# The router ahead of the expert passes: a shorter chain to the positions, expert weights from ranks, unread products in TensorE's holes

## The reference, cut to what matters

```python
p_group = softmax(t @ wg_r + bg_r)                 # 4 groups
g_val, g_idx = top_k(p_group, 1)
e_logits = (t @ we_r + be_r).reshape(-1, 4, 4)     # 4 experts in each group
sel = e_logits[token, g_idx]                       # the 4 logits of the own group
top_v, top_i = top_k(sel, 2)
top_w = softmax(top_v)                             # weights of the two best experts
combine = one_hot(g_idx) * g_val  x  top_w at top_i
for e in range(16):
    out += combine[:, e] * ((silu(t @ w_gate[e]) * (t @ w_up[e])) @ w_down[e])
```

## Time and profile before

| what | us |
|---|---|
| median of 3 runs | 1613.51 |
| lowest and highest run | 1607.58, 1614.62 |
| span of the profiled execution | 1608.3 |
| TensorE busy in it | 1567.1 |

### The profile page before, as it was taken

One profiled execution on the slowest core, in us unless ns is written; L12 is line 12 of the kernel. 1 busy time (PEld: TensorE's weight loads), 2 busy tenths in 40 slices (PEclk: granted clock), 3 DMA queues, 4 the chain that ended last, 5 costly groups with the idle time before them and its releaser, 6 DMA issues.

```text
span 1608.3 us, 29082 instructions
## 1 busy us (share of the span) xinstructions
PE 1567.1 (97%) x11814; PEld 1471.9 (92%) x11814; DVE 1138.0 (71%) x1424; ACT 855.9 (53%) x1056; POOL 63.4 (4%) x53
## 2 busy tenths in 40 slices
PE   6999999999999999999999999999999989999998
PEld 6999998889999999998888999989999978888886
DVE  7655587766555765569777655578688679889887
ACT  5534454664433643345566433376445467767765
POOL 0000021000000000002100000020210000000000
PEclk9999999999999999999999999999999999999999
DMA  8666744136565576674315555646543759898992
GB/s 274 206 197 186 184 142 125 44 123 209 184 201 183 178 222 196 188 182 131 110 55 182 176 191 183 189 131 185 157 123 114 261 202 359 318 361 317 340 343 101
DMA packets 243781, 311.64 MB, mean 194 GB/s; under 512 B 51940, under 2 KB 183588, under 8 KB 243700
## 3 DMA queue, kind: packets, MB, share of 16 engines
q1 hardware_dynamic: 243088, 309.57, 60.1%
q10 hardware_dynamic: 612, 0.96, 0.2%
HBM read 306.97 MB, written 1.05 MB: 192 GB/s over the span
## 4 chain that ended last, share of the span: by engine, by line
PE 86%; DVE 7%; ACT 4%; DVEq 2%; issue 1%; DMA 1%; SPq 0%; ACTq 0%
PE psum L412 20%; PE psum L414 20%; PE psum L413 20%; PE psum L2740 3%; PE psum L2739 3%; PE psum L2741 3%; PE psum L2765 2%; PE psum L2766 2%; PE psum L2767 2%; DVE unit_low L404 2%; ACT unit_high L398 1%; PE psum L2685 1%; PE psum L1020 1%; PE psum L903 1%; DVEq L2247 1%
## 5 line engine op out<-in xcount | busy, mean ns | idle before, releaser
L404 DVE TENSOR_TENSOR unit_low<-unit_raw,unit_high 128x2048 fp32r<-128x2048 f32 (+1 forms) x186 | 425.8, 2291 | 208.5 <-ACT unit_high L398 208.4
L398 ACT ACTIVATE unit_high<-unit_raw 128x2048 fp32r<-128x2048 f32 (+1 forms) x186 | 346.9, 1869 | 134.0 <-PE psum L414 133.5
L412 PE MATMUL psum<-UH,unit_high 128*128 128x256 f32 x1120 | 319.4, 285 | 6.4 <-DVE UL L458 4.6
L413 PE MATMUL psum<-UL,unit_high 128*128 128x256 f32 x1120 | 316.1, 282 | 0.0
L414 PE MATMUL psum<-UH,unit_low 128*128 128x256 f32 x1120 | 315.8, 282 | 0.0
L2476 DVE TENSOR_TENSOR unit_low<-unit_raw,unit_high 128x2048 fp32r<-128x2048 f32 x96 | 215.5, 2285 | 20.8 <-ACT unit_high L2472 20.7
L412 PEld LDWEIGHTS psum<-UH,unit_high 128*128 128x128 f32 x1120 | 213.2, 190 | 9.2 <-DVE unit_low L404 5.2
L414 PEld LDWEIGHTS psum<-UH,unit_low 128*128 128x128 f32 x1120 | 213.2, 190 | 0.0
L413 PEld LDWEIGHTS psum<-UL,unit_high 128*128 128x128 f32 x1120 | 212.4, 190 | 0.1
L412 PE MATMUL psum<-U2H,unit_high 128*128 128x256 f32 x704 | 197.1, 280 | 1.4 <-DVE U2L L458 1.2
L413 PE MATMUL psum<-U2L,unit_high 128*128 128x256 f32 x704 | 196.3, 279 | 0.0
(11 more groups left out here) (501 smaller groups left out, 2913.4 us busy)
## 6 DMA issues: line engine op xcount, KB each, us to landing
unit_raw<-in_ffn_wg SPq DMA_DIRECT2D x44, 1024.0 KB
unit_raw<-in_ffn_wu SPq DMA_DIRECT2D x44, 1024.0 KB
unit_raw<-in_ffn_wd SPq DMA_DIRECT2D x44, 1024.0 KB
unit_raw<-in_w_in SPq DMA_DIRECT2D x32, 1024.0 KB
unit_raw<-in_expert_w_gate SPq DMA_DIRECT2D x32, 1024.0 KB, 7.2
unit_raw<-in_expert_w_up SPq DMA_DIRECT2D x32, 1024.0 KB, 8.1
unit_raw<-in_expert_w_down SPq DMA_DIRECT2D x32, 1024.0 KB, 6.7
unit_raw<-in_w_out SPq DMA_DIRECT2D x10, 1024.0 KB
```

The costliest lines, as they stand in the source:

```text
L398: act.activation(high[s][:, 0:w], raw[s][:, 0:w], ACT.Copy).then_inc(unit_high, 1)
L404: dve.tensor_tensor(low[s][:, 0:w], raw[s][:, 0:w], high[s][:, 0:w].bitcast(F32), ALU.subtract).then_inc(unit_low, 1)
L412: pe.matmul(dst, wh, xh, start=start, stop=False, skip_group_check=True)
L413: pe.matmul(dst, wh, xl, start=False, stop=False, skip_group_check=True)
```

## The change

Nine things change:

- `first_max` goes. For the group, the comparison with the maximum and the multiplication by the tie weights become one instruction for each of the two token tiles, and the last comparison writes `OH` itself. A second one writes the same to `RT`.
- The gathering of the own group's expert logits (a product of 32 values and a sum) moves from the chain of positions to after `plan`. A maximum over the four and a subtraction join it there, all ahead of the split of unit 1.
- TensorE gets unread products of 128x512 (in `router_pe`): six after the logits, three after the counts, three after the gather. Nobody reads what they write.
- The exponential is one instruction for both softmaxes, after ScalarE's evacuation of both halves instead of ahead of the split of unit 2, and the second one is gone.
- VectorE evacuates both halves and then splits unit 2 (before: half, unit 2, half).
- VectorE splits unit 4 ahead of the weights.
- The weights: an expert is kept when fewer than two others rank above it; its weight is its exponential over the sum of the kept ones. 12 instructions in place of 22.
- In the first pass TensorE gathers the weights between units 4 and 5, instead of after unit 3. Other passes are as before.
- The constants have 16 more columns.

```diff
+            def unread_products(n):
+                for _ in range(n):
+                    pe.matmul(psum[:, 1, :], high_x[0][:, 0:P], high_x[0][:, 0:512], start=True, stop=True, skip_group_check=True)
+            unread_products(6)
             pe.wait_ge(EM.sem, EM.at("group"))
...
+            unread_products(3)
             pe.wait_ge(EM.sem, EM.at("position"))
...
             gather_pe(pe, 0)
+            unread_products(3)
...
             expert_high(act, 0, G2, 1, used(G2, EU - 1))
-            act.wait_ge(EM.sem, EM.at("g_sub"))
-            act.activation(RT[:, :, 24:28], RT[:, :, 24:28], ACT.Exp).then_inc(BM.sem, BM.inc("g_exp"))
             expert_high(act, 0, G2, 2)
             evacuate_act(act, 0)
+            act.wait_ge(EM.sem, EM.at("g_sub"))
+            act.activation(RT[:, :, 24:32], RT[:, :, 24:32], ACT.Exp).then_inc(BM.sem, BM.inc("g_exp"))
             expert_high(act, 0, G2, 3)
             expert_high(act, 0, G2, 4)
-            act.wait_ge(EM.sem, EM.at("t_sub"))
-            act.activation(RT[:, :, 84:85], RT[:, :, 84:85], ACT.Exp).then_inc(BM.sem, BM.inc("t_exp"))
...
-            first_max(c(0, 4), 20, 28, 22, 32)
-            dve.drain()
-            dve.tensor_copy(OH[:, :, :], c(32, 36)).then_inc(EM.sem, EM.inc("group"))
-            dve.tensor_tensor(c(24, 28), c(0, 4), wide(20), ALU.subtract).then_inc(EM.sem, EM.inc("g_sub"))
+            dve.tensor_reduce(c(20), c(0, 4), AX, ALU.max)
+            dve.drain()
+            for n in range(2):
+                dve.scalar_tensor_tensor(out=RT[:, n, 28:32], in0=RT[:, n, 0:4], scalar=RT[:, n, 20:21], in1=K[:, K_TIE],
+                                         op0=ALU.is_ge, op1=ALU.mult)
+            dve.drain()
+            dve.tensor_reduce(c(22), c(28, 32), AX, ALU.max)
+            dve.drain()
+            dve.tensor_tensor(OH[:, :, :], c(28, 32), wide(22), ALU.is_equal).then_inc(EM.sem, EM.inc("group"))
+            dve.tensor_tensor(c(32, 36), c(28, 32), wide(22), ALU.is_equal)
...
             dve.drain().then_inc(EM.sem, EM.inc("plan"))
+            dve.tensor_tensor(c(24, 28), c(0, 4), wide(20), ALU.subtract)
+            dve.tensor_tensor(c(40, 56).rearrange(four, g=4), ...)
+            dve.drain()
+            dve.tensor_reduce(c(56, 60), c(40, 56).rearrange("p n (g e) -> p n e g", g=4), AX, ALU.add)
+            dve.drain()
+            dve.tensor_reduce(c(60), c(56, 60), AX, ALU.max)
+            dve.drain()
+            dve.tensor_tensor(c(28, 32), c(56, 60), wide(60), ALU.subtract).then_inc(EM.sem, EM.inc("g_sub"))
             expert_low(dve, G2, 1)
-            evacuate_dve(dve, 0, lambda: expert_low(dve, G2, 2))
+            evacuate_dve(dve, 0)
+            expert_low(dve, G2, 2)
             expert_low(dve, G2, 3)
+            expert_low(dve, G2, 4)
+            # is_gt, is_ge, times K_LESS, max, sum: the rank of each of the four
...
             dve.wait_ge(BM.sem, BM.at("g_exp"))
-            # the two first maxima of the four expert logits and their weights: 22 instructions
+            dve.scalar_tensor_tensor(out=c(112, 116), in0=c(96, 100), scalar=1.5, in1=c(28, 32), op0=ALU.is_lt, op1=ALU.mult)
+            # two sums, product, reciprocal, times RS[2:4], times the kept exponentials
...
             dve.wait_ge(QM.sem, QM.at("position_b"))
             dve.tensor_copy(POSB[:, :], psum[:, 3, 0:T])
-            expert_low(dve, G2, 4)
...
-            def projection(bank, g, j, kind, q):
+            def slot_weights():
+                pe.wait_ge(EM.sem, EM.at("comb"))
+                ...
+            def projection(bank, g, j, kind, q, first=False):
                 for u in range(2):
+                    if first and j == 1 and kind == 0 and u == 1:
+                        slot_weights()
```

More of the change, by code:

```diff
@@ L92 @@
 K_IOTAC = _take(1)
+K_LESS = _take(16)
 K_COLS = _off
@@ L128, in constants @@
     c[:, K_IOTAC] = i[:, None]
+    c[:, K_LESS] = (i[None, 0:4] < i[0:4, None]).astype(np.float32).reshape(1, 16)
     c[:, K_TIE] = np.array([4, 3, 2, 1], np.float32)
@@ L1634, in build @@
                       "sc3", "yo2", "yd2", "yt2", "yz2", "scn2", "yn2", "sc_low2", "scn3", "sc_low3", "uly2"]
-                   + ["ss_sum", "group", "g_sub", "position", "plan", "t_sub", "comb"])
+                   + ["ss_sum", "group", "position", "plan", "g_sub", "comb"])
         HM = Marks(sem("hybrid_pool"), ["res", "dt_s", "dA", "xdec0", "xdec1", "xd1", "sdec", "yz1", "xd2"])
@@ new lines, in router_dve @@
+            own_ = c(56, 60).unsqueeze(3).to_broadcast([P, 2, 4, 4])
+            dve.tensor_tensor(c(64, 80).rearrange(four, g=4), other, own_, ALU.is_gt)
+            dve.tensor_tensor(c(80, 96).rearrange(four, g=4), other, own_, ALU.is_ge)
+            dve.drain()
+            dve.tensor_tensor(c(80, 96), c(80, 96), K[:, K_LESS].unsqueeze(1).to_broadcast([P, 2, 16]), ALU.mult)
+            dve.drain()
+            dve.tensor_tensor(c(64, 80), c(64, 80), c(80, 96), ALU.max)
+            dve.drain()
@@ L2638, in router_dve @@
+            dve.tensor_reduce(c(96, 100), c(64, 80).rearrange(four, g=4), AX, ALU.add)
+            dve.drain()
             dve.wait_ge(BM.sem, BM.at("g_exp"))
-            dve.tensor_reduce(c(23), c(24, 28), AX, ALU.add)
+            dve.scalar_tensor_tensor(out=c(112, 116), in0=c(96, 100), scalar=1.5, in1=c(28, 32), op0=ALU.is_lt, op1=ALU.mult)
+            dve.tensor_reduce(c(117), c(24, 28), AX, ALU.add)
             dve.drain()
-            dve.reciprocal(c(23), c(23))
+            dve.tensor_reduce(c(116), c(112, 116), AX, ALU.add)
@@ L2642, in router_dve @@
             dve.drain()
-            dve.tensor_tensor(RT[:, :, 23], RT[:, :, 23], RS[:, 2:4], ALU.mult)
-            first_max(c(56, 60), 60, 64, 61, 68)
+            dve.tensor_tensor(c(118), c(116), c(117), ALU.mult)
             dve.drain()
-            dve.tensor_scalar(c(72, 76), c(68, 72), 3 * NEG, None, ALU.mult)
+            dve.reciprocal(c(118), c(118))
             dve.drain()
-            dve.tensor_tensor(c(72, 76), c(72, 76), c(56, 60), ALU.add)
+            dve.tensor_tensor(RT[:, :, 119], RT[:, :, 118], RS[:, 2:4], ALU.mult)
@@ L2649, in router_dve @@
             dve.drain()
[L2650 to L2665, removed]
+            dve.tensor_tensor(c(92, 96), c(112, 116), wide(119), ALU.mult).then_inc(EM.sem, EM.inc("comb"))
             dve.wait_ge(QM.sem, QM.at("position_b"))
             dve.tensor_copy(POSB[:, :], psum[:, 3, 0:T])
-            expert_low(dve, G2, 4)
@@ L2698, in evacuate_act, with evacuate_dve @@
                 ins.then_inc(ug_high, 1)
-        def evacuate_dve(dve, q, between=lambda: None):
+        def evacuate_dve(dve, q):
             for half in range(2):
-                if half:
-                    between()
                 dve.wait_ge(ug_high, 2 * q + (half + 1))
@@ L2727, in expert_pe @@
             last = (GROUPS - 1) + pe.value_load(PLAN[0:1, 0:1], min_val=0, max_val=1)
-            def projection(bank, g, j, kind, q):
+            def slot_weights():
+                pe.wait_ge(EM.sem, EM.at("comb"))
+                for n in range(2):
+                    mm = pe.matmul(psum[:, W_B, 0:4], SEL[:, n, :], RT[:, n, 92:96], start=(n == 0), stop=(n == 1))
+                mm.then_inc(w_gathered, 1)
+            def projection(bank, g, j, kind, q, first=False):
                 for u in range(2):
+                    if first and j == 1 and kind == 0 and u == 1:
+                        slot_weights()
                     e = unit_of(j, kind, u)
@@ L2783, in one_pass @@
                     pe.wait_ge(silu, 4 * q + (EB + j))
-                    projection(G_B, g, j, 0, q)
+                    projection(G_B, g, j, 0, q, first)
                     transposes(j - 1, q)
```

20 lines of the change are left out of this document (5 added, 15 removed).

## The result

The changed kernel took 1613.71 us (median of 20 runs, 1611.52 to 1618.78), the kernel before 1607.78 (median of 20 runs beside them; one of these took 3951.4 us, the other 19 took 1607.07 to 1614.62). The ratio is 1.0029, 95% interval 1.0022 to 1.0036: 4.7 us slower. That is inside the 0.5% that I had called no change, but it is a real loss, on the side that I had not forecast.

What follows compares the result with a forecast made beforehand. It took TensorE's chain of waits through the router to bound the kernel. The terms 1.42 + 0.4 + 1.59 - 0.44 - 0.3 = 2.67 us, taken off the 1613.5 median, gave 1610.8, range 1604.8 to 1614.6.

Steps and rivals of the forecast that it cites:

- the sum: Router to unit 6: earlier start 1.42, `UL` wait 0.4, unit 4 wait 1.59, less gather 0.44 and stall 0.3: 2.67 us.
- shifts that no row speaks of: Leftover case for effects nowhere in the profile rows, given no size; chance 0.03.
- The chain to the positions: Router, group's maximum to positions: `OH` comes 0.33 us earlier, everything up to L2676 about 0.37 us earlier.
- The unread products and the gather: Router: unread products fill TensorE's holes, the clock stays up, and the gather's second half ends at 1300.0 instead of 1303.0.
- What is late next: Start of first pass: unit 1's split starts 0.5 us later than before, yet TensorE begins 1.42 us earlier.
- The first 48 products, the weights, their gather: First pass: products take 11.3 us, not 11.70; unit 4's wait goes; gather costs 0.44 us; unit 6 stalls 0.3 us.
- The clock falls all the same: Rival in the router: the clock drops despite unread products, TensorE begins 0.3 to 0.9 us later, median 1611.4; chance 0.33.
- Transfers or splits hold the passes: Rival in the passes: loads or VectorE set the pace, TensorE stalls later by what it won, time stays 1613.5; chance 0.11.
- The weights come late: Rival in the first pass: TensorE waits for `comb`, slower if later than 1318.4, median 1614.5 at 1 us beyond; chance 0.03.

Runs made afterwards that it cites:

- Experiments 1: The kernel before with only the 16 unread columns of constants, tiles behind `K` 64 bytes further: 1616.04 us, ratio 1.0038.
- experiment 5: The changed kernel with the tiles behind `K` 192 bytes further, 256 bytes in all from their old place: 1606.85 us, ratio 0.9987.
- experiment 7: The kernel before with the 16 unread columns and the tiles behind `K` 256 bytes from their old place: 1609.78 us, ratio 0.9997.
- experiment 4: The changed kernel with tiles behind `K` 64 bytes further still (128 in all) and without its twelve unread products: 1614.56 us, ratio 1.0033.
- Experiment 6: experiment 5 with the expert-logit instructions between VectorE's evacuation halves and unit 6 split before the wait for the weights: 1606.21 us, ratio 0.9976.
- experiment 3: The changed kernel with the tiles behind `K` 32 bytes further, 96 bytes in all from their old place: 1613.22 us, ratio 1.0025.
- experiment 11: experiment 5 with the weights' gather back in its old place after unit 3, one execution: 1605.71 us.
- experiment 12: Experiment 6 with the weights' gather back after unit 3 and unit 6's split behind the wait again: 1606.07 us, ratio 0.9982.

## Why the prediction was wrong, step by step

**The step that failed** is one sentence of the sum: "The moved instructions and the 16 columns of constants are in these steps or under them". For the instructions that held. The columns I costed at nothing, since no engine works on them for long. I didn't follow what they push along. I had every tile behind `K` in the code in front of me, and no entry for their addresses in the sum, only 0.03 for "shifts that no row speaks of". The entry should have been about +6.5 us, what the 2112 products of `U2H` and `U2L` took more. Experiments 1, 5 and 7 show it: the columns without the rest cost 6.1, with the shift brought to 256 bytes they cost nothing that can be told from zero, and the changed kernel then gains 2.1.

**The base was off too.** I subtracted 2.67 from 1613.5, the median of three runs. The median of 20 is 1607.8. The span of 1608.3 that I had for the profiled execution pointed lower than 1613.5: time less span is 1.8 us in all later profiled executions, which makes 1610.1. That is still 2.3 above the median, but 5.2 us between the median of three and this span were a sign that two of the three runs were high, and not something to add to the forecast. The forecast of 1610.8 came near 1613.7 by luck, by two errors that partly cancel: a base 5.7 too high and a missing loss.

**The chain to the positions:** right. Forecast 0.33 for `OH` and 0.37 for the positions; measured 0.30 and 0.33.

**The unread products and the gather:** right for this execution. The clock stayed at 1.00, the holes are 0.8, 0.6 and 0.3 where I had 1.0, 0.8 and 0.6, and the 32 products took 3.54 from first to last start. Without the unread ones unit 6 comes 1.0 later (experiment 4). That the clock stays up was luck in part: in three of seven executions it didn't.

**What is late next:** right. The split of unit 1 starts 0.61 later against the common point (forecast 0.5), TensorE waits for `UL` behind it, and starts 1.38 earlier (forecast 1.42). Experiment 6 removes that wait and gets 0.68 more at the same place (17.53 to 16.85).

**The first 48 products, the weights, their gather:** from the first product to the weights' gather 14.01 us passed (forecast 14.13); the wait for unit 4 is gone; TensorE never waits for `comb`. The gather costs 0.36 in its new place, where I took 0.44. VectorE goes from the copy to unit 6's split in 0.97 (0.96), and TensorE loses 0.25 to it (the four transposes to unit 6 take 0.60, before 0.35), where I had 0.3.

**Sum:** 2.79 against 2.67, in experiment 5 2.78, each against the profiled execution of the kernel before. Against experiment 7, where the clock cost less, it would be 1.97.

**The rivals.** *The clock falls all the same* is true of some executions, as I had said of it: three of seven, at nothing in experiment 3, at 0.6 us in experiment 11, inside my 0.3 to 0.9, and 1.6 in experiment 12, outside it. "TensorE: Matmul & The Clock Gate", Part 1, of the Trainium skill says that the monitor runs freely, and the traces agree: the same program ahead of the gather (experiments 5 and 11) gave a clock of 1.00 in one execution and 0.50 in the other. *Transfers or splits hold the passes* is refuted: 286.09 us from unit 6 to the end in both kernels. *The weights come late* didn't happen. The case that decided was in none of them.

**What stays open.** Whether the operands and the weights that TensorE reads at the same time collide in SBUF, or either with VectorE, ScalarE or the transfers, no run here tells apart. Nor is it shown why `U2H`, `U2L`, `YH` and `YL` react to a shift of 64 bytes and `UNH` and `UNL`, which moved as far, don't (124.0 ns before and after), or whether 256 is the period or only one good distance. The time at 128 bytes is not accounted for by the step. The difference of medians (5.9 us, 4.7 by the ratio) is larger than that of the two profiled spans (3.0), because the profiled execution of the kernel before, at 1610.1, was 2.3 slower than its median, and that of the changed kernel 0.6 faster. Executions of one kernel differ by several microseconds in where the clock falls, and one profile of each can't say what the rest is.

## What to carry to other kernels

Count a new column, constant or buffer as a move of every tile laid out behind it: compare how many matmuls go into equal windows of unedited code before anything else, and separate the move from the edit before judging the edit itself (here 256 bytes in all brought the old step back, and 96 and 128 didn't). A local gain is read from a common point just ahead of the edit, not from the end of the span. And when only three runs are known, hold the base of a forecast against the profiled execution's span plus its constant extra (1.8 us here); in this case that came 2.3 us from the median of 20, and the median of three 5.7.

## What the runs showed of the hardware

- The step of a 128x256 fp32r product in a stream without waits can depend on where the moving operands of the stream lie against the other tiles, the weight units among them: 116.8 to 120.1 ns between shifts of 0 and 64 bytes a partition for `U2H` and `U2L`, 116.8 again at 256 bytes, with TensorE "busy" 100% in each case. It doesn't for every tile: `UNH` and `UNL` kept 124.0 ns at 64 bytes. Moving all of them together by 64 bytes changes nothing (116.8).
- Moving one operand (`U2L`, 64 bytes) slows the products next to it that don't read it, by 0.9 ns each. `HH`, which didn't move, ran faster between products of tiles that did (117.9 to 116.5 ns).
- The steps have a pattern and no scatter: in the changed kernel long stretches repeat 121, 117, 125, 116, 123, 118 ns, where the kernel before repeats 117, 116, 117.
- Unread 128x512 products in the holes go with a rarer fall of the clock and don't exclude it: it fell in the router in seven of seven profiled executions without them and in three of seven with them.
